# A hybrid decoder step on eight cores: weights converted by their transfers, norm weights multiplied into the normed rows, x loaded first

## The chip, the cores and the metric

The kernel runs as one program on the 8 cores of one Trainium2 chip. Each core takes one of the 8 prompt sequences and 16 of the 128 decode sequences, and no data goes between cores. The metric is device time in microseconds (us) of the slowest core. TensorE (PE) multiplies, VectorE (DVE) and ScalarE (ACT) do the elementwise work, GpSimd (POOL) builds masks and issues the transfers of its queue, SyncE (SP) issues most transfers.

## What is computed

One layer: an RMS norm, one joint input projection, two head groups in parallel (a gated linear recurrence, HGRN2, and sliding-window attention with a sink), an output projection with residual, a second norm, an MLP with squared ReLU, a last norm.

```python
def _rmsnorm(x, g):
    y = x * rsqrt(mean(x * x, -1) + EPS)
    return y * g

xn = _rmsnorm(h, ln_mix)
zq, zf, zi, zg, sq, sk, sv = split(xn @ w_in)
o_hg = rmsnorm_per_head(gla(zq, zf, zi), hg_norm) * silu(zg)
h = h + concat([o_hg, swa(sq, sk, sv, sinks)]) @ w_out
u = _rmsnorm(h, ln_mlp) @ w_up
h = h + square(relu(u)) @ w_down
y = _rmsnorm(h, ln_final)
```

x is f32, 4096 rows of 1024 per core for the prompt and 128 rows for the decode tokens. All weights come as f32; products are made in bf16.

## The kernel before

The 32 tiles of 128 prompt rows form 8 groups of 4 tiles (512 rows). The weights are 24 chunks, `wall`, of 128 x 4096 elements: 2 MB in f32, 1 MB in bf16. Chunks 0 to 5 are the input projection, 6 and 7 the output projection, 8 to 15 the up and 16 to 23 the down projection. Every group needs every chunk again, so each chunk is converted once: its bf16 form is written to `wbf` in DRAM and read back from there into a ring of 5 SBUF slots `s_wr` (`w_load`, `w_prefetch`, `w_use`, `w_release`).

The conversion goes in quarters of a chunk. `q_issue` loads 512 KB of f32 into one of four staging buffers (in `M`) on SP's queue. `q_cast` makes bf16 of it, quarters 0 and 2 on ScalarE (lines 396, 404), 1 and 3 on VectorE (lines 399, 406), and multiplies the norm weight of each row in on the way (`ln_mix`, `hg_norm`, `ln_mlp`), so that the norms themselves only scale by the inverse root. The result goes into the slot, or, for chunks that are converted ahead of use (`qc["conv"]`), into the x buffers `s_xt` and from there to `wbf`. `store` writes a slot's bf16 to `wbf`. `tick()`, called after each step of the schedule, advances this by one quarter or one store. Engines run their instructions in program order, so a cast whose quarter has not landed holds all behind it on its engine.

Order of work (`main_schedule`): (a) norms of group 0, then the input projections of groups 0 and 1 together (`head_steps`), with the norms of group 1 (`second_norms`) among them; the gate arithmetic (`gate`) runs on DVE and ACT beside the later projections. (b) Attention of group 0 alone (`back`): nothing for TensorE to do beside it. (c) For each group g: the MLP of g (`mlp_steps`) is interleaved with the attention of g+1 and the input projection of g+2 (`second`); the norms of g+2 read x tiles from `s_xt` (`xt_load`), and the residual tiles of g+2 come by `load_x`. The decode tokens ride along in group 3. Line 617 and 619 make the inverse root, line 615 the sum of squares, line 626 the scaled rows, line 633 turns them, line 635 evicts them. Line 644 and 651 are the projections and the up projection, 1247 the down projection, 1081 the output projection.

Of the kernel before, what the change touches and what calls it, by code (L numbers as in the profile page):

```python
# [6 lines left out]
F32 = mybir.dt.float32  # L7
# [159 lines left out]
def build_program(worder=None, weights=None):  # L167
# [3 lines left out]
    nc = bass.Bass("TRN2", target_bir_lowering=False, dynamic_dma_scratch_size=2048)  # L171
# [13 lines left out]
    lnmix_d = din("lnmix", [128, 8])  # L185
    lnmlp_d = din("lnmlp", [128, 8])
# [99 lines left out]
    MBYTES = 37 * 1024 + 256  # L286
    M = nc.alloc_sbuf_tensor("M", [128, MBYTES // 2], BF16)
    stg_cv = Carver(M[:, :], MBYTES)
    stg32 = [stg_cv.take([2, 512], F32) for i in range(4)]
# [46 lines left out]
    pool1(lambda e: e.affine_select(out=C.seqmask[:, :], in_=C.seqmask[:, :], pattern=[[8, 16]], base=7,
                                    channel_multiplier=-1, compare_op=ALU.is_ge, fill=0.0), [C.seqmask])
    pool1(lambda e: e.memset(C.wos[:, :], 1.0), [C.wos])
    for c in range(4):
        P.op("dve", lambda e, c=c: e.tensor_copy(out=C.wos[:, c:c + 1], in_=C.hgn[:, 0:1]), reads=[C.hgn], writes=[C.wos])  # L340
    P.op("dve", lambda e: e.tensor_tensor(out=C.dl[:, :], in0=C.lbl[:, 0:4], in1=C.lbl[:, 4:8], op=ALU.subtract),
         reads=[C.lbl], writes=[C.dl])
    P.op("act", lambda e: e.activation(out=C.lb[:, :], in_=C.dl[:, :], func=AF.Sigmoid), reads=[C.dl], writes=[C.lb])
    P.op("dve", lambda e: e.tensor_scalar(out=C.oml[:, :], in0=C.lb[:, :], scalar1=-1.0, scalar2=1.0, op0=ALU.mult,
                                          op1=ALU.add), reads=[C.lb], writes=[C.oml])
    P.op("dve", lambda e: e.tensor_scalar(out=C.noml[:, :], in0=C.lb[:, :], scalar1=-1.0, scalar2=None, op0=ALU.add),
         reads=[C.lb], writes=[C.noml])
    P.op("act", lambda e: e.activation(out=C.esinkT[:, :], in_=C.sinkT[:, :], func=AF.Exp), reads=[C.sinkT],
         writes=[C.esinkT])
    P.op("act", lambda e: e.activation(out=C.esinkB[:, :], in_=C.esinkB[:, :], func=AF.Exp), writes=[C.esinkB])  # L350
    P.op("dve", lambda e: e.tensor_scalar(out=C.homl[:, :], in0=C.oml[:, :], scalar1=0.5, scalar2=None, op0=ALU.mult),
# [29 lines left out]
    def q_cast():  # L381
# [27 lines left out]
        elif qi == 3:  # L409
            stores.append([cid, s_, 2])  # L410
# [1074 lines left out]
```

How the kernel before makes its waits and increments, by code:

```python
    def _wait(self, e, tok):  # L65
        if tok is None:
            return
        sn, v = tok
        if e is self.E["pe"] and sn == "e_pe":
            return
        if e.waited.get(sn, 0) >= v:
            return
        e.h.wait_ge(self.sems[sn], v)
        e.waited[sn] = v
# [23 lines left out]
    def op(self, en, fns, reads=(), writes=()):  # L98
        e = self.E[en]
        if callable(fns):
            fns = [fns]
        self._deps(e, reads, writes)
        ins = None
        for f in fns:
            ins = f(e.h)
        ins.then_inc(self.sems[e.semname], 1)
        e.n += 1
        tok = (e.semname, e.n)
        self._mark(tok, reads, writes)
        return tok
# [1 line left out]
    def dma(self, out, in_, reads=(), writes=(), sem=None, q="sp"):  # L112
        e = self.E[q]
        sem = sem + "_" + q
        self.dsem(sem)
        self._deps(e, reads, writes)
        ins = e.h.dma_start(out=out, in_=in_)
        ins.then_inc(self.sems[sem], 16)
        self.dcnt[sem] += 16
        tok = (sem, self.dcnt[sem])
        self._mark(tok, reads, writes)
        return tok
```

## Time and profile before

| | us |
|---|---|
| median of 3 runs | 1708.95 |
| lowest, highest | 1702.04, 1713.07 |
| the profiled execution | 1703.14 |
| its span on the slowest core (7) | 1702.1 |
| spans of the other cores | 1680.2 to 1698.6 |
| PE busy | 1537.5 (90%) |
| ACT busy, DVE busy | 961.6 (56%), 739.0 (43%) |
| DMA, mean | 183 GB/s |

"Busy" is the time in which an engine runs an instruction; matmul ends are modelled. PEclk in the rows is the granted TensorE clock as a share of 2.4 GHz. In brackets stand the idle time ahead of an instruction and what ended it. The page shows the span in 40 slices; in tenths, TensorE is busy 4785589969 in the first ten (425 us) and 8 to 9 in nearly all the rest.

### The profile page before, as it was taken

What the parts mean: (1) busy time and instruction counts of PE and PEld (TensorE: products, weight loads), DVE (VectorE), ACT (ScalarE), POOL (GpSimd) and SP (SyncE); (2) the same over time, 40 slices, a digit from 0 to 9 for tenths busy, and PEclk for the clock granted to TensorE, in tenths of its full rate; (3) what the DMA queues carried; (4) which work ended last, traced back from release to release, by engine and by line L of the source; (5) the groups of instructions that cost most, each with busy time, mean ns of one, the idle gap of its engine ahead of it and who ended that gap; (6) DMA issues with size and microseconds to landing.
All of it is one profiled execution on the core that took longest, in us unless ns stands there. A gap on an engine that the chain in (4) does not pass through costs nothing.

```text
span 1702.1 us, 26771 instructions; the slowest of 8 cores (1680.2 to 1702.1 us)
## 1 busy us (share of the span) xinstructions
PE 1537.5 (90%) x8883; PEld 745.6 (44%) x8883; DVE 739.0 (43%) x1305; ACT 961.6 (56%) x1767; POOL 76.3 (4%) x140
## 2 busy tenths in 40 slices
PE   4785589968999998899899999999999999999997
PEld 2333344423444544444455554444444444444443
DVE  2256635523544164664444435444254425343222
ACT  4656556655555655455665556555665566554433
POOL 1000000000201000110000000000000000000000
PEclk9896789988999999999999999999999999999998
DMA  8786986965745537652464334944464334634541
GB/s 242 211 266 220 250 227 230 293 201 198 260 153 139 168 106 251 216 174 87 173 213 152 118 116 163 266 176 146 164 232 173 110 151 160 227 125 168 205 154 50
DMA packets 72710, 312.01 MB, mean 183 GB/s; under 512 B 12000, under 2 KB 21216, under 8 KB 48736
## 3 DMA queue, kind: packets, MB, share of 16 engines
q1 hardware_dynamic: 46672, 257.33, 46.0%
q0 software_dynamic: 17456, 48.77, 8.3%
q10 hardware_dynamic: 8448, 4.20, 0.9%
q8 instruction: 75, 1.23, 0.3%
q14 instruction: 59, 0.48, 0.1%
HBM read 264.13 MB, written 49.15 MB: 184 GB/s over the span
## 4 chain that ended last, share of the span: by engine, by line
PE 69%; ACT 10%; DMA 8%; issue 6%; DVE 5%; SPq 0%; ACTq 0%; DVEq 0%; POOL 0%; POOLq 0%
PE pb L644 31%; PE pb L1247 24%; PE pb L1081 6%; DMA M<-wall 5%; ACT s_junk L615 2%; PE pb L651 2%; ACT s_rl L1229 2%; PE pb L633 1%; DMA s_wr<-wbf 1%; DVE XR L1251 1%; DMA wbf<-s_xt 1%; DVE U L798 1%; PE pb L904 1%; PE pb L954 1%; DMA ss<-M 1%
## 5 line engine op out<-in xcount | busy, mean ns | idle before, releaser
L644 PE MATMUL pb<-s_hnT,s_wr 128*128 128x512 bf16 x2184 | 511.5, 384 | 11.4 <-ACT M L685 3.6
L1247 PE MATMUL pb<-s_wr,s_aT 128*128 128x512 bf16 x2048 | 479.0, 382 | 25.1 <-ACT s_aT L1232 15.7
L644 PEld LDWEIGHTS pb<-s_hnT,s_wr 128*128 128x128 bf16 x2184 | 209.0, 99 | 256.3 <-issue 32.4
L1247 PEld LDWEIGHTS pb<-s_wr,s_aT 128*128 128x128 bf16 x2048 | 194.9, 98 | 262.8 <-issue 52.3
L1251 DVE TENSOR_TENSOR XR<-pb,XR 128x512 f32<-128x512 f32 x256 | 175.9, 688 | 205.0 <-PE pb L1247 197.1
L644 PE MATMUL pb<-s_xnT,s_wr 128*128 128x512 bf16 x952 | 228.8, 393 | 29.2 <-DMA s_wr<-wbf 10.1
L1229 ACT ACTIVATE s_rl<-pb 128x512 bf16<-128x512 f32 (+1 forms) x288 | 159.8, 555 | 164.6 <-PE pb L644 157.8
L1232 ACT ACTIVATE s_aT<-s_rl 128x512 bf16<-128x512 bf16 x256 | 161.2, 630 | 23.5
L644 PEld LDWEIGHTS pb<-s_xnT,s_wr 128*128 128x128 bf16 x952 | 94.0, 100 | 143.7 <-issue 46.1
L1081 PE MATMUL pb<-s_wr,s_omT 128*128 128x512 bf16 x512 | 130.0, 400 | 7.6 <-ACT s_omT L931 7.5
L615 ACT ACTIVATE s_junk<-XR 128x1024 bf16<-128x1024 f32 x72 | 75.8, 1053 | 74.3 <-DVE XR L1251 67.4
L626 DVE TENSOR_SCALAR s_xnb<-XR,s_rs 128x1024 bf16<-128x1024 f32 x40 | 30.2, 755 | 145.9 <-ACT s_rs L619 145.9
L961 ACT ACTIVATE U<-pb 128x512 bf16<-128x512 f32 x126 | 67.7, 588 | 37.6 <-PE pb L954 34.7
L1081 PEld LDWEIGHTS pb<-s_wr,s_omT 128*128 128x128 bf16 x512 | 51.2, 102 | 71.8 <-issue 19.7
L1269 DVE SCALAR_TENSOR_TENSOR XR<-XR,s_rs,s_gfin 128x1024 f32<-128x1024 f32 x32 | 41.1, 1285 | 82.4 <-ACT s_rs L619 80.0
L1084 DVE TENSOR_TENSOR XR<-pb,XR 128x512 f32<-128x512 f32 x64 | 44.1, 688 | 74.0 <-PE pb L1081 73.7
L633 PE MATMUL pb<-s_ident,s_xnb 128*128 128x128 bf16 x528 | 43.3, 229 | 35.0 <-DVE s_xnb L626 32.1
L651 PE MATMUL pb<-s_wr,s_xnT 128*128 128x512 bf16 (+2 forms) x448 | 65.9, 303 | 7.1 <-ACT U L742 4.2
L633 PEld LDWEIGHTS pb<-s_ident,s_xnb 128*128 128x128 bf16 x528 | 36.4, 102 | 50.4 <-issue 39.1
L840 ACT ACTIVATE U<-pb,s_epsc 128x512 f32<-128x512 f32 x33 | 22.5, 682 | 56.2 <-PE pb L838 49.8
L117 POOL DMA_DIRECT2D y<-XR x32 | 17.4, 543 | 818.7 <-DVE XR L1269 301.4
L685 ACT ACTIVATE U<-pb 128x512 bf16<-128x512 f32 x56 | 33.2, 596 | 36.4 <-PE pb L644 35.5
(209 smaller groups left out, 1457.5 us busy)
## 6 DMA issues: line engine op xcount, KB each, us to landing
s_wr<-wbf SPq DMA_DIRECT2D x167, 1024.0 KB, 5.9
M<-wall SPq DMA_DIRECT2D x96, 512.0 KB, 8.7
wbf<-s_wr SPq DMA_DIRECT2D x19, 1024.0 KB, 8.8
y<-XR POOLq DMA_DIRECT2D x32, 512.0 KB, 3.6
s_xt<-x POOLq DMA_DIRECT2D x24, 512.0 KB, 6.0
XR<-x POOLq DMA_DIRECT2D x24, 512.0 KB, 7.5
wbf<-s_xt SPq DMA_DIRECT2D x20, 256.0 KB, 7.2
XR<-x SPq DMA_DIRECT2D x8, 512.0 KB, 12.6
```

The lines of the kernel that those rows point to most:

```text
L615: P.op("act", lambda e: e.activation(out=junk[:, :], in_=src[:, :], func=AF.Square, accum_out=ssq[:, 0:1]), reads=[src], writes=[ssq, junk])
L633: P.op("pe", [lambda e, k=k: e.transpose(bkb[:, k * 128:(k + 1) * 128], xb[:, k * 128:(k + 1) * 128], C.ident[:, :]) for k in range(8)], r ...
L644: P.op("pe", [lambda e, k=k: e.matmul(bk[0:ncols, 0:TB], lhsT=W[:, k, col0:col0 + ncols], rhs=srcT[:, k, 0:TB], start=(k == 0), stop=(k == ...
L651: P.op("pe", [lambda e, k=k: e.matmul(bk[:, 0:ncols], lhsT=srcT[:, k, j * 128:(j + 1) * 128], rhs=W[:, k, c0:c0 + ncols], start=(k == 0), ...
L961: P.op("act", lambda e, pt=pt, bk=bk: e.activation(out=pt[:, :], in_=bk[:, :], func=AF.Exp, scale=0.125), reads=[bk], writes=[pt])
L1081: P.op("pe", [lambda e, k=k: e.matmul(bk[:, :], lhsT=B.omT[:, k, j * 128:(j + 1) * 128], rhs=W[:, k, :], start=(k == 0), stop=(k == 7)) fo ...
L1084: P.op("dve", lambda e: e.tensor_tensor(out=xs_[:, nh * 512:(nh + 1) * 512], in0=bk[:, :], in1=xs_[:, nh * 512:(nh + 1) * 512], op=ALU.add ...
L1229: P.op("act", lambda e, bk=bk, rl=rl, TB=TB: e.activation(out=rl[:, 0:TB], in_=bk[:, 0:TB], func=AF.Relu), reads=[bk], writes=[rl])
L1232: P.op("act", lambda e, fl=fl, rl=rl, TB=TB, B=B: e.activation(out=B.aT[:, fl, 0:TB], in_=rl[:, 0:TB], func=AF.Square), reads=[rl], writes ...
L1247: P.op("pe", [lambda e, f=f, B=B, j=j, W=W, bk=bk: e.matmul(bk[:, :], lhsT=B.aT[:, f, j * 128:(j + 1) * 128], rhs=W[:, f, :], start=(f == ...
L1251: P.op("dve", lambda e, nh=nh, bk=bk, xs_=xs_: e.tensor_tensor(out=xs_[:, nh * 512:(nh + 1) * 512], in0=bk[:, :], in1=xs_[:, nh * 512:(nh ...
L1269: P.op("dve", lambda e: e.scalar_tensor_tensor(out=xs_[:, :], in0=xs_[:, :], scalar=rs[:, 0:1], in1=C.gfin[:, :], op0=ALU.mult, op1=ALU.mu ...
```

## The change

1. Conversion. Staging buffers, `q_issue`, `q_cast` and all casts on ScalarE and VectorE go. `w_load` of a chunk that is not converted yet is one transfer on POOL's queue, f32 in DRAM to the bf16 slot; the store to `wbf` stays. 11 chunks go this way. The other 13 are converted by `convert()`: one transfer on POOL's queue from `wall` to `wbf`, DRAM to DRAM, one at every third step of stage (b); POOL waits ahead of it for all of TensorE's work so far and for the last transfer but one.
2. Norm weights. `norm_pre` multiplies the full f32 row `gmix` or `gmlp` (128 x 1024, loaded on ACT's queue) in with a scalar_tensor_tensor instead of the tensor_scalar; `hg_norm` is multiplied in where `t1` is made, by another scalar_tensor_tensor. The sum of squares writes its unused output into `s_xnb` instead of `s_junk`.
3. Start. Four x tiles are the first issues of SP; the small constants follow. POOL issues the first two chunks ahead of its constants, the next three behind them. The ops on the gate constants come behind group 0's norms.
4. x tiles of groups 2 and (residuals) 2 go on SP's queue instead of POOL's. The decode tokens' x comes through `s_xt` and once more into `M` for the residual.
5. Smaller masks for the decode tokens, broadcast in the instruction. The descriptor scratch of POOL's queue is doubled, `M` is 7 KB smaller.

```diff
-    nc = bass.Bass("TRN2", target_bir_lowering=False, dynamic_dma_scratch_size=2048)
+    nc = bass.Bass("TRN2", target_bir_lowering=False, dynamic_dma_scratch_size=4096)
...
         if cid in converted:
...
+            P.dma(dst, wbf_d[cid], reads=[wbfb[cid]], writes=[wring[s_]], sem="wr%d" % s_)
         else:
             converted.add(cid)
-            qload.extend((cid, s_, qi) for qi in range(4))
-            while qload and len(qcast) < 4:
-                q_issue()
+            P.dma(dst, wall_d[cid], writes=[wring[s_]], sem="wc%d" % s_, q="pool")
+            stores.append([cid, s_, 2])
+
+    def convert():
+        for cid in WORDER[wr["next"]:]:
+            if cid not in converted:
+                converted.add(cid)
+                e = P.E["pool"]
+                P._wait(e, ("e_pe", P.E["pe"].n))
+                if len(straight) > 1:
+                    P._wait(e, straight[-2])
+                straight.append(P.dma(wbf_d[cid], wall_d[cid], writes=[wbfb[cid]], sem="cd%d" % (len(straight) % 2),
+                                      q="pool"))
+                return
...
-    def norm_pre(src):
-        rs = norm_stats(src)
+    def norm_pre(src, gain):
...
         xb = xnb[xnb_free.pop(0)]
-        P.op("dve", lambda e: e.tensor_scalar(out=xb[:, :], in0=src[:, :], scalar1=rs[:, 0:1], scalar2=None,
-                                              op0=ALU.mult), reads=[src, rs], writes=[xb])
+        rs = norm_stats(src, xb)
+        P.op("dve", lambda e: e.scalar_tensor_tensor(out=xb[:, :], in0=src[:, :], scalar=rs[:, 0:1], in1=gain[:, :],
+                                                     op0=ALU.mult, op1=ALU.mult), reads=[src, rs, gain], writes=[xb])
...
         xs[0] = [load_x(n) for n in gtiles(0)]
+        P.dma(C.gmix.ap, gmix_d, writes=[C.gmix], sem="gmix", q="act")
+        w_prefetch(2)
+        const_ops()
         w_prefetch()
+        const_loads()
         xs[1] = [load_x(n) for n in gtiles(1)]
...
-        tk["every"] = 2
         qc["conv"] = True
```

The rows of the program show the places. First SP at the start of the program, in the form of a difference (- before, + after; `XR` holds the residual tiles of x):

```order
-L117 DMA s_lnmix<-lnmix 128x8
-L117 DMA s_lnmlp<-lnmlp 128x8
+L117 DMA XR<-x 128x1024 x4
 L117 DMA s_lbl<-lbl 128x8
 L117 DMA s_hgn<-hgn 128x1
@@ -6,77 +5,20 @@
 L117 DMA s_esinkB<-sinkB 128x8
 L117 DMA XR<-x 128x1024 x4
-L117 DMA M<-wall 128x1024 x4
-L117 DMA XR<-x 128x1024 x4
-L117 DMA M<-wall 128x1024 x6
```

The first four x tiles moved from behind six small transfers to the front, and the f32 quarters (`M<-wall`) left SP. Next POOL in the changed kernel, from its last start constant to its first transfers in stage (c):

```order
L331 MEMSET s_S_bf 128x512
L117 DMA s_wr<-wall 128x4096 x9
L117 DMA wbf<-wall 32x16384 x13
L117 DMA s_xt<-x 128x1024 x2
L117 DMA s_gfin<-gfin 128x1024
```

Where POOL had no transfer before stage (c), it now has 22; each direct one is written as 32 rows of 16384 elements, 64 KB of f32 each. Last ScalarE in stage (b), attention of the first tiles, before:

```order
L404 CAST s_xt<-M 128x1024
L833 ACTIVATE U<-pb 128x512
L881 CAST s_S_bf<-Sst 128x512
L404 CAST s_xt<-M 128x1024
L829 COPY U<-pb 128x512
L615 ACTIVATE s_junk,s_ssq<-XR 128x1024
L617 ACTIVATE s_tv<-s_ssq,s_epsc 128x1
```

and the same place in the changed kernel:

```order
L771 ACTIVATE U<-pb 128x512
L819 CAST s_S_bf<-Sst 128x512
L767 COPY U<-pb 128x512
L545 ACTIVATE s_xnb,s_ssq<-XR 128x1024
L547 ACTIVATE s_tv<-s_ssq,s_epsc 128x1
```

The two weight casts (`s_xt<-M`) are gone; the rest stands in the same order. TensorE's rows are the same in both kernels throughout, up to line numbers.

## Rows read from the trace of the kernel before

**Rows 1.** Table by stretches of the slowest core: busy us of each engine, instructions.

```profile
core 7: us, PE busy (x) PEld busy (x) DVE busy (x) ACT busy (x) POOL busy (x), PEclk, DMA share, GB/s
...
150.00:225.00 75.00, 43.33 (x265) 22.95 (x263) 42.78 (x92) 39.85 (x71) 0.00 (x0) 0.68 0.88 249
...
340.00:400.00 60.00, 41.24 (x177) 17.76 (x176) 13.86 (x24) 32.38 (x48) 0.98 (x2) 0.77 0.65 215
...
450.00:1702.00 1252.00, 1193.63 (x7060) 583.01 (x7059) 544.12 (x940) 699.85 (x1314) 58.80 (x99) 0.99 0.48 164
```

**Rows 2.** Timeline, first 60 us: start, length, engine, line, instruction, [idle before <-releaser].

```profile
1.05 0.39 SPq L117 DMA_DIRECT2D s_lnmix<-lnmix  x1
...
3.86 1.94 SPq L117 DMA_DIRECT2D XR<-x  x4
...
16.17 1.04 ACT L615 ACTIVATE s_junk<-XR 128x1024 bf16<-128x1024 f32 x1
...
20.18 0.69 DVE L635 COPY s_xnT<-pb 128x1024 bf16<-128x1024 bf16 x1 [0.67 <-PE pb L633]
...
24.22 9.88 PE L644 MATMUL pb<-s_xnT,s_wr 128*128 128x512 bf16 x32 [4.15 <-DVE s_wr L399]
...
37.41 4.97 PE L644 MATMUL pb<-s_xnT,s_wr 128*128 128x512 bf16 x16 [3.31 <-DVE s_wr L399]
...
58.28 1.01 PE L633 MATMUL pb<-s_ident,s_xnb 128*128 128x128 bf16 x8 [4.30 <-DVE s_xnb L626]
```

**Rows 3.** Timeline, 104 to 225 us: end of the gate arithmetic, a cast on ScalarE.

```profile
105.64 3.27 PE L644 MATMUL pb<-s_hnT,s_wr 128*128 128x512 bf16 x8 [3.55 <-ACT M L685]
...
148.10 0.88 DVE L399 TENSOR_SCALAR s_wr<-M,s_lnmlp 128x512 bf16<-128x512 f32 x2 [2.23 <-ACT s_wr L396]
...
149.33 0.58 PE L819 MATMUL pb<-U 128*128 128x128 bf16 x4 [1.87 <-DVE s_vS_all L775]
...
159.13 1.04 ACT L404 CAST s_wr<-M 128x1024 bf16<-128x1024 f32 x1 [5.50 <-DMA M<-wall]
```

**Rows 4.** Groups by line, 150 to 225 us: weight casts of ScalarE and VectorE.

```profile
L396 ACT ACTIVATE s_xt<-M,s_lnmlp 128x512 bf16<-128x512 f32 x8 | 5.3, 714 | 5.3 <-DMA wbf<-s_xt 5.3
L404 ACT CAST s_xt<-M 128x1024 bf16<-128x1024 f32 x5 | 5.2, 1045 | 5.6 <-DMA wbf<-s_xt 5.6
...
L399 DVE TENSOR_SCALAR s_xt<-M,s_lnmlp 128x512 bf16<-128x512 f32 x8 | 3.5, 480 | 0.0
```

**Rows 5.** Timeline, 350 to 400 us: a cast on ScalarE and the three stops of TensorE.

```profile
355.77 1.04 ACT L404 CAST s_wr<-M 128x1024 bf16<-128x1024 f32 x1 [7.77 <-DMA M<-wall]
...
358.60 6.50 PE L644 MATMUL pb<-s_xnT,s_wr 128*128 128x512 bf16 x16 [8.45 <-ACT s_aT L1232]
...
380.57 3.57 PE L644 MATMUL pb<-s_xnT,s_wr 128*128 128x512 bf16 x8 [5.12 <-DMA s_wr<-wbf]
389.33 3.57 PE L1247 MATMUL pb<-s_wr,s_aT 128*128 128x512 bf16 x8 [5.19 <-DVE s_wr L406]
```

**Rows 6.** Page, DMA queues, q1: packets, MB, share of 16 engines.

```profile
q1 hardware_dynamic: 46672, 257.33, 46.0%
```

**Rows 7.** DMA view, 542 to 544 us: the cache loads that convert f32 to bf16.

```profile
q0 software_dynamic: 997, 0.29, 129.4%
```

**Rows 8.** DMA view, 1078 to 1082 us: two queues at once.

```profile
q1 hardware_dynamic: 108, 0.78, 71.9%
q0 software_dynamic: 93, 0.38, 23.6%
```

**Rows 9.** DMA view, 1084 to 1092 us: DRAM to DRAM copies in q1.

```profile
q1 hardware_dynamic: 39, 1.29, 72.3%
```

**Rows 10.** Timeline, 248 us: first norm of the third group of tiles.

```profile
248.40 1.06 ACT L615 ACTIVATE s_junk<-s_xt 128x1024 bf16<-128x1024 f32 x1 [0.70 <-DMA s_xt<-x]
```

**Rows 11.** Page, costliest groups: norm scaling and final norm on VectorE.

```profile
L626 DVE TENSOR_SCALAR s_xnb<-XR,s_rs 128x1024 bf16<-128x1024 f32 x40 | 30.2, 755 | 145.9 <-ACT s_rs L619 145.9
...
L1269 DVE SCALAR_TENSOR_TENSOR XR<-XR,s_rs,s_gfin 128x1024 f32<-128x1024 f32 x32 | 41.1, 1285 | 82.4 <-ACT s_rs L619 80.0
```

More of the change, by code:

```diff
@@ L285, in build_program @@
     rl_p = [sb("rl%d" % i, [512], BF16) for i in range(2)]
-    MBYTES = 37 * 1024 + 256
+    MBYTES = 30 * 1024 + 256
     M = nc.alloc_sbuf_tensor("M", [128, MBYTES // 2], BF16)
-    stg_cv = Carver(M[:, :], MBYTES)
-    stg32 = [stg_cv.take([2, 512], F32) for i in range(4)]
     UBYTES = 37 * 1024
@@ L336, in build_program @@
[L336 to L349, printed above, removed]
@@ L381, in q_cast @@
-    def q_cast():
-        cid, s_, qi, st = qcast.pop(0)
-        sc = C.lnmix if cid < 6 else (C.wos if cid < 8 else (C.lnmlp if cid < 16 else None))
-        en = ("act", "dve")[qi % 2]
-        if s_ is None:
-            dst = cq[qc["c"] % 4]
-            while any(t_[1] is None and t_[4] is dst for t_ in stores):
-                store(stores.pop(0))
-            qc["c"] += 1
-            dap = dst.ap
-        else:
-            dst = wring[s_]
-            dap = dst[:, 2 * qi:2 * qi + 2, :]
-        if sc is not None:
-            if en == "act":
-                fns = [lambda e, k=k: e.activation(out=dap[:, k, :], in_=st[:, k, :], func=AF.Identity,
-                                                   scale=sc[:, 2 * qi + k:2 * qi + k + 1]) for k in range(2)]
-            else:
-                fns = [lambda e, k=k: e.tensor_scalar(out=dap[:, k, :], in0=st[:, k, :],
-                                                      scalar1=sc[:, 2 * qi + k:2 * qi + k + 1], scalar2=None,
-                                                      op0=ALU.mult) for k in range(2)]
-            P.op(en, fns, reads=[st, sc], writes=[dst])
-        elif en == "act":
-            P.op(en, lambda e: e.copy(out=dap, in_=st[:, :, :]), reads=[st], writes=[dst])
-        else:
-            P.op(en, lambda e: e.tensor_copy(out=dap, in_=st[:, :, :]), reads=[st], writes=[dst])
-        if s_ is None:
-            stores.append([cid, None, 2, qi, dst, (qc["c"] - 1) % 4])
-        elif qi == 3:
-            stores.append([cid, s_, 2])
@@ L434, in w_load @@
         cid = WORDER[l]
-        while any(q[0] == cid for q in qload + qcast):
-            q_step()
         if any(wslot_free[0] == t_[1] or t_[0] == cid for t_ in stores):
@@ L473, in tick @@
         w_prefetch()
-        if qc["conv"] and not qload and not record:
-            for cid in WORDER[wr["next"]:]:
-                if cid not in converted:
-                    converted.add(cid)
-                    qload.extend((cid, None, qi) for qi in range(4))
-                    break
-            while qload and len(qcast) < 4:
-                q_issue()
+        if qc["conv"] and not record and tk["i"] % tk["every"] == 0:
+            convert()
     def w_use(cid):
@@ L493, in w_use @@
             wr["next"] += 1
-        while any(q[0] == cid for q in qload + qcast):
-            q_step()
         w_prefetch()
@@ L524, in carve @@
         K.rd8 = two.take([8], F32)
+        K.kt_smp = two.take([512], BF16)
         share(one, two)
```

264 lines of the change are left out of this document (124 added, 140 removed).

## The prediction

> **What bounds the kernel now.** I read four views. The table by stretches comes first: from 450 us to the end TensorE is busy 1193.6 of 1252 us at a granted clock of 0.99 of full speed [rows 1]. The TensorE rows stand in the same order in both kernels, so nothing is to be had there, about three quarters of the time. In 150 to 225 us, attention of group 0 alone, TensorE is busy 43.3 of 75 us at 0.68, VectorE 42.8 and ScalarE 39.9: no engine is full, so a chain of operations from engine to engine sets the pace. In 340 to 400 us TensorE is busy only 41.2 of 60 us, at 0.77. The time to be had lies in the first 400 us.
>
> The timeline says what the chain waits for there. The first projection, at 24.22, waited for a weight cast on VectorE though the last normed rows were evicted at 20.87; the second chunk's, at 37.41, waited 3.31 us for one too; at 58.28 a transpose waited 4.30 us for normed rows that stood behind casts [rows 2]. At 105.64 TensorE waited 3.55 us for an eviction that ScalarE had behind a cast whose f32 quarter was late [rows 3]. In stage (b) ScalarE stood still 5.5 us at 159.13 for a quarter [rows 3], and 5.3 and 5.6 us for staging space whose store to `wbf` was not through [rows 4]. From 350 to 390 the same thing comes three times: a cast waits 7.77 us for its quarter, the eviction behind it is late, TensorE stops for 8.45, 5.12 and 5.19 us [rows 5]. The waits come from casts that stand in the program order of two engines ahead of work that others need.
>
> **The change part by part.** I count against the profiled execution (1703.14; the median is 1708.95, so 5.8 is added at the end).
>
> *Start.* The first x tiles were issued at 3.86 behind six small transfers, the first of them at 1.05 [rows 2]; now they lead, 2.8 us earlier. But `wall` and `gmix` now come beside them from another queue. The main queue moves 257.33 MB in 46.0% of 16 engines' 1702 us, 20.5 GB/s an engine, 330 on 16 [rows 6]. If the queues share by bytes, 2.1 MB of x, as much of `wall` and 0.5 of `gmix` land at 3 + 4.7/0.33 = 17.3. From the last Square to the end of the last eviction it was 16.17 to 20.87, 4.7 us [rows 2]; the scaling becomes a scalar_tensor_tensor, whose nearest row takes 1285 ns against 755 [rows 11], so 5.2. First projection at 22.6 instead of 24.22: **-1.6**. The second chunk is then there: **-3.3**. Casts among the second norms: three stops of 3 to 4.3 us [the longest in rows 2], of which the slower scaling and the later x tiles leave most; I take **-3.0** and not 10.
>
> *Gates, 105 to 149.* The 3.55 us at 105.64 go. Between 105 and 150 stand 12 casts of 0.48 on VectorE and 13 of 0.71 on ScalarE (durations of rows 4), 5.8 and 9.2 us, in a chain that uses both engines by turns; half of them, 7.3, is on it. The end waits for `s_vS_all` behind two halves at 148.10 [rows 3], 3.5 us. Sum **-14.4**.
>
> *Attention of group 0.* The 5.5 us at 159.13 go whole. Of the 10.9 us behind staging stores [rows 4] I take 6, since some fall where ScalarE had nothing due. Cast time is 5.3 + 5.2 on ScalarE, 3.5 on VectorE for the half shown and about as much for the plain casts, with those into slots some 22 us; a quarter on the chain, 5.5. Sum **-17**. The bounds are 5.5 (only the first wait counts) and 5.5 + 10.9 + 22 = 38 (everything was on it).
>
> *Stage (c).* The stops sum to 18.8 us; behind them 32 matmuls went in 6.50 + 3.57 + 3.57 = 13.6 us, 0.43 each [rows 5], which is the low clock (the mean granted clock of the stretch is 0.77 [rows 1]); at the full one they take half, so 6.8 more. 25.6 together; I take **-24**. By then all weights are converted, if the direct transfers are done.
>
> *What it adds.* 66 scalings (two for each of 32 tiles and for the decode tokens) cost 0.53 us each more [rows 11]; VectorE has the room beside the MLP (544 of 1252 us busy [rows 1]). Where a head waits for a norm, in the first tiles, some count: **+3**; if no cover were left it would be 35. `t1` by scalar_tensor_tensor and `hg_norm`: the same element count as before, nothing; its cover is TensorE waiting elsewhere. Contention of the new traffic with loads that TensorE needs: **+2**, a choice between nothing and the first rival. x tiles 1 and 2 of group 2 now stand on SP behind two slot loads that wait for TensorE's release; SP has nothing else due, and the tiles were needed at 248.40 [rows 10], so nothing. Masks and constants are off the path.
>
> *The direct transfers.* This is the price that no row has. 13 chunks go from f32 to bf16 DRAM to DRAM in rows of 64 KB, two per engine and chunk, one every third step from about 147 us; the first x tile of group 2 would be wanted at 248.4 less what was gained, 22, so at 226. The nearest row for the rate: cache loads that convert write 0.29 MB in 2 us with the queue full [rows 7], 0.58 MB of f32 read, 290 GB/s, 7.2 us for 2 MB. 13 x 7.2 = 94 us of engine time from 147 on: end at 241 if nothing else ran. The other traffic of stage (b) is small, and x tiles don't wait for the conversions if queues share by bytes. From rows the two queues share packet by packet: 93 packets of 4.1 KB in one beside 108 of 7.2 KB in the other, 4 us, both with work [rows 8]. The Trainium skill, DMA: Bandwidth & Descriptors, "Queues, rings and completion order", says the same, that an engine takes turns between queues a packet at a time; by that rule, were a 64 KB row one packet, the forecast turns into the first rival. What the forecast rests on is that the software queue cuts its rows: the mean packet there is 4.1 KB though rows are 4 KB, which fits both. I give cutting into small pieces a bit over half.
>
> Sum: -1.6 -3.3 -3.0 -14.4 -17 -24 +3 +2 = -58.3, so 1644.8 for a profiled execution and **1650** for the median. Own range: -47 with attention at -5.5; -76 with attention at -27 (all waits, half the cast time) and the second norms at -10. On the median's scale 1633 to 1662.
>
> **The rivals.** *Big packets.* If rows of 16 KB and 64 KB are one packet each, every 4 KB packet of x waits for 16 KB of weights: 0.8 + 0.2 us at 20.5 GB/s, 32 times per engine, x lands at 3 + 32 = 35 and the first projection starts at 40. All five chunks are there, so no more stops: the gates end some 5 us earlier than before, not 22. The direct rows: copies of 61 KB in the main queue give 39 packets, 1.29 MB, 72.3% of 8 us, 2.4 us each and, with 18 big and 21 small of 0.43, 4.6 us for a big one [rows 9]. A round of one 64 KB row and one 8 KB packet takes 3.6 us (3.2 + 0.4 at 20.5 GB/s) up to 5.0 (4.6 + 0.4). 26 rounds end at 147 + 26r: 241 to 277. The x tiles of group 2 sit behind two slot loads in the main queue, 16 + 16 rounds, so land about 3 us behind the end of all conversions. First norm at 244 to 280 instead of 226, and the sum is -22 (start to attention) -24 +3 +(18 to 54) = -25 to +11: 1684 to 1720, middle 1700. For it: rows 9 has such packets as wholes. Against: those are of the hardware queue.
>
> *Slower.* The same mechanism with a dearer round, since f32 to bf16 in DRAM writes back what it reads. It decides at 269 us, r = 4.7: there the gain is used up. Over r = 5.4 (end at 287) it is more than 1% slower, 1726; at 6.2 the end is 308 and the time 1748. Loads of `s_wr` that cross it come over 20 us after issue, since all of their eight packets an engine then wait for a 64 KB row each. No row excludes a round of 6.2.
>
> *Half.* Both waits shrink but the chain of gates and attention is its own bound: attention -5.5, gates -7, stops -17, the rest as above: 1674.
>
> *The change does nothing for the stops.* `s_wr` loads come late by the direct transfers instead of by casts. Then -58.3 + 24 = -34, again near 1674; I put it with *Half*.
>
> **How the numbers follow.** Forecast 0.52, big packets 0.24, slower 0.13, half 0.11. A measurement of this kernel can tell 1% from no change, 17 us: below 1692 is faster, above 1726 slower. Faster: 0.52 + 0.11 and of big packets only where r is below 3.9, 0.03: 0.66. Same: 0.21. Slower 0.13. The range goes from 1634 over the half case into big packets up to 1706, which leaves out the slower rival and the upper third of big packets.
>
> **What would show it.** Right: the first L644 matmul (new number of the line) near 22 us and no stop at the second chunk; packets of the software queue of 4 KB while `wall` loads; no cast of `M` on ScalarE or VectorE; stage (b) of 55 to 60 us at a clock above 0.68; no TensorE stop above 3 us between 330 and 400; the first norm of group 2 near 226. Wrong: packets of 16 or 64 KB in the software queue and the first projection at 40 us; `s_xt<-x` on SP landing over 20 us after issue, and TensorE idle ahead of group 2's transposes; `wbf<-wall` still running at 250. The prediction falls with the step on how rows are cut.

## The result

The changed kernel takes 1724.01 us against 1708.10 before, medians of seven runs each. In some executions, whichever the kernel, the cores of one die run at a lower clock and the time is longer; all ratios, and all times from here on, leave these out, and since the profiled execution of the changed kernel is one of them (cores 4 to 7), its rows are read on core 0 (span 1717.9). The ratio is 1.0079, with a 95% interval of 1.0053 to 1.0105: 0.8% slower, 13.5 us (about 1720 against 1708). The forecast was 1650, with a range to 1706. The time lies outside it, on the other side of before. The first rival, big packets (1684 to 1720), comes nearest, right where it meets the second (slower, from 1726 on).

Where times of before and after are set beside each other below, both are core 0's, unless core 7 is named. The page first (it is that of the slowest core, 4; core 0 has the same packets): the two queues, q1 the main one of SP and q0 that of POOL (packets, MB, share of the engines), then issues with KB each and median us to landing.

```profile
q1 hardware_dynamic: 30832, 205.94, 34.1%
q0 software_dynamic: 18656, 70.26, 18.3%
...
wbf<-wall POOLq DMA_DIRECT2D x13, 1024.0 KB, 20.9
s_wr<-wall POOLq DMA_DIRECT2D x11, 1024.0 KB, 13.0
wbf<-s_wr SPq DMA_DIRECT2D x11, 1024.0 KB, 22.2
```

The main queue moves 51 MB less than in [rows 6], and a conversion takes 13 to 21 us to land. The table by stretches of core 0:

```profile
core 0: us, PE busy (x) PEld busy (x) DVE busy (x) ACT busy (x) POOL busy (x), PEclk, DMA share, GB/s
...
150.00:225.00 75.00, 57.84 (x349) 28.84 (x347) 34.64 (x67) 33.90 (x65) 2.95 (x6) 0.81 1.01 128
225.00:340.00 115.00, 52.35 (x266) 23.29 (x263) 24.97 (x46) 23.86 (x46) 2.46 (x5) 0.72 0.77 144
340.00:400.00 60.00, 57.15 (x355) 28.44 (x354) 24.83 (x43) 34.59 (x62) 1.61 (x3) 1.00 0.39 139
...
450.00:1702.00 1252.00, 1206.49 (x7146) 588.52 (x7144) 569.11 (x946) 708.62 (x1328) 56.12 (x99) 0.99 0.50 168
```

Two stretches have improved as forecast. In 150 to 225 TensorE is busy 57.8 us at 0.81 (before 43.8 at 0.72; core 7 in [rows 1] 43.3 at 0.68), and in 340 to 400 57.2 us at 1.00 (before 38.5 at 0.80; core 7 41.2 at 0.77): attention is faster and the three stops of [rows 5] are gone. But in 225 to 340 TensorE is busy 52.4 of 115 us, where core 0 before had 111.0. What stands there:

```profile
291.45 1.06 ACT L545 ACTIVATE s_xnb<-s_xt 128x1024 bf16<-128x1024 f32 x1 [66.19 <-DMA s_xt<-x]
...
232.58 3.57 PE L1187 MATMUL pb<-s_wr,s_aT 128*128 128x512 bf16 x8 [5.68 <-DMA s_wr<-wbf]
...
295.41 1.18 PE L893 MATMUL pb<-M,s_kT_all 64*128 64x512 bf16 x2 [56.60 <-DVE XR L1191]
```

ScalarE waited 66.2 us for the first x tile of group 2, and TensorE stood still 56.6 us behind it. Before, core 0 began this norm at 242.96. A loss at the start is seen in the timeline too: the four first norms, an activation on the constants, the first norm of group 1, then the first projection and the transposes behind that norm.

```profile
7.92 1.06 ACT L545 ACTIVATE s_xnb<-XR 128x1024 bf16<-128x1024 f32 x1
...
14.82 1.06 ACT L545 ACTIVATE s_xnb<-XR 128x1024 bf16<-128x1024 f32 x1 [5.02 <-DMA XR<-x]
...
23.23 1.06 ACT L545 ACTIVATE s_xnb<-XR 128x1024 bf16<-128x1024 f32 x1 [6.57 <-DMA XR<-x]
...
31.18 1.06 ACT L545 ACTIVATE s_xnb<-XR 128x1024 bf16<-128x1024 f32 x1 [6.12 <-DMA XR<-x]
...
47.13 0.20 ACT L334 ACTIVATE s_esinkT<-s_sinkT 128x4 f32<-128x4 f32 x1 [14.13 <-DMA s_esinkB<-sinkB]
...
52.71 1.05 ACT L545 ACTIVATE s_xnb<-XR 128x1024 bf16<-128x1024 f32 x1
...
36.49 13.46 PE L574 MATMUL pb<-s_xnT,s_wr 128*128 128x512 bf16 x48 [0.94 <-DVE s_xnT L565]
...
57.34 1.01 PE L563 MATMUL pb<-s_ident,s_xnb 128*128 128x128 bf16 x8 [7.39 <-DVE s_xnb L556]
```

The four x tiles come 7 to 8 us apart and the first projection starts at 36.49 instead of 25.07 (core 0 before; 24.22 on core 7, [rows 2]). Then ScalarE stands 14.1 us for the small constants, which were issued by 5.6 us. The norms of group 1 stand behind them in its program, and TensorE stops for these, 7.4 us at 57.34.

A ledger of one core shows where time is won and lost. Each line is the start of the same sum of squares in both timelines of core 0 (the how-manieth of 99, and what it reads):

| norm | before | after | difference |
|---|---|---|---|
| 4, last tile of group 0 | 17.02 | 31.18 | +14.2 |
| 8, last tile of group 1 | 53.49 | 64.24 | +10.7 |
| 12, last one of attention of group 0 | 214.78 | 195.82 | -19.0 |
| 13, first x tile of group 2 | 242.96 | 291.45 | +48.5 |
| 17 | 308.47 | 357.95 | +49.5 |
| 23 | 429.58 | 453.73 | +24.2 |
| 95 | 1570.28 | 1598.12 | +27.8 |

So: 14 lost at the start, 30 won between 53 and 215 us, 67 lost at one x tile, 25 won at the stops. Everything that the casts cost was given back, as forecast; two waits for x took more.

The end of this ledger, +27.8, is twice the 13.5 us of the whole. The metric is the slowest core, and core 0 before was not it (1690.1 us, core 7 1702.1), while core 0 after is the longest of its die. The ledger tells where time goes; the size of the whole is the ratio's to tell.

### The profile page after: what moved, and what is told of

The parts are those of the page before. It is cut to its first block, busy times and chain, and to the rows that moved or that the text cites. A ratio compares the mean times of both kernels' runs of the same rounds, so it can differ in the third digit from the quotient of the medians.

```text
span 1783.1 us, 26077 instructions; the slowest of 8 cores (1705.9 to 1783.1 us)
## 1 busy us (share of the span) xinstructions
PE 1582.6 (89%) x8713; PEld 762.1 (43%) x8883; DVE 737.0 (41%) x1221; ACT 910.2 (51%) x1687; POOL 78.9 (4%) x153
## 4 chain that ended last, share of the span: by engine, by line
PE 73%; ACT 8%; DMA 5%; DVE 5%; issue 4%; another core or an unknown queue 4%; ACTq 0%; SPq 0%; DVEq 0%; POOL 0%; POOLq 0%
PE pb L574 34%; PE pb L1187 24%; PE pb L1021 7%; DMA s_esinkB<-sinkB 2%; PE pb L581 2%; DMA s_wr<-wbf 1%; ACT s_xnb L545 1%; PE pb L563 1%; ACT s_rl L1169 1%; DVE U L730 1%; PE pb L893 1%; PE pb L842 1%; DMA ss<-M 1%; ACT s_aT L1172 1%
## 5 line engine op out<-in xcount | busy, mean ns | idle before, releaser
L574 PE MATMUL pb<-s_hnT,s_wr 128*128 128x512 bf16 x2126 | 527.2, 398 | 12.9 <-ACT U L771 2.5
L1187 PE MATMUL pb<-s_wr,s_aT 128*128 128x512 bf16 x1986 | 501.8, 401 | 26.8 <-ACT s_aT L1172 11.5
L574 PEld LDWEIGHTS pb<-s_hnT,s_wr 128*128 128x128 bf16 x2184 | 215.0, 101 | 268.4 <-issue 108.4
L1187 PEld LDWEIGHTS pb<-s_wr,s_aT 128*128 128x128 bf16 x2048 | 202.3, 102 | 281.4 <-issue 140.8
L1172 ACT ACTIVATE s_aT<-s_rl 128x512 bf16<-128x512 bf16 x256 | 161.2, 630 | 24.7 <-ACT s_rl L1169 1.5
L545 ACT ACTIVATE s_xnb<-XR 128x1024 bf16<-128x1024 f32 x72 | 75.9, 1054 | 94.2 <-DVE XR L1191 69.1
L556 DVE SCALAR_TENSOR_TENSOR s_xnb<-XR,s_rs,s_gmlp 128x1024 bf16<-128x1024 f32 x32 | 41.1, 1283 | 122.4 <-ACT s_rs L549 122.4
L900 ACT ACTIVATE U<-pb 128x512 bf16<-128x512 f32 x126 | 67.9, 589 | 40.9 <-PE pb L893 39.1
L556 DVE SCALAR_TENSOR_TENSOR s_xnb<-s_xt,s_rs,s_gmix 128x1024 bf16<-128x1024 f32 x25 | 32.1, 1284 | 131.7 <-ACT s_rs L549 131.7
L563 PEld LDWEIGHTS pb<-s_ident,s_xnb 128*128 128x128 bf16 x528 | 37.9, 105 | 72.6 <-issue 63.6
L581 PE MATMUL pb<-s_wr,s_xnT 128*128 128x128 bf16 (+2 forms) x447 | 66.1, 306 | 0.1
L545 ACT ACTIVATE s_xnb<-s_xt 128x1024 bf16<-128x1024 f32 x25 | 26.2, 1047 | 66.0 <-DMA s_xt<-x 66.0
```

The costliest lines, as they stand in the source:

```text
L545: P.op("act", lambda e: e.activation(out=scrap[:, :], in_=src[:, :], func=AF.Square, accum_out=ssq[:, 0:1]), reads=[src], writes=[ssq, scrap])
L556: P.op("dve", lambda e: e.scalar_tensor_tensor(out=xb[:, :], in0=src[:, :], scalar=rs[:, 0:1], in1=gain[:, :], op0=ALU.mult, op1=ALU.mult) ...
L563: P.op("pe", [lambda e, k=k: e.transpose(bkb[:, k * 128:(k + 1) * 128], xb[:, k * 128:(k + 1) * 128], C.ident[:, :]) for k in range(8)], r ...
L574: P.op("pe", [lambda e, k=k: e.matmul(bk[0:ncols, 0:TB], lhsT=W[:, k, col0:col0 + ncols], rhs=srcT[:, k, 0:TB], start=(k == 0), stop=(k == ...
L581: P.op("pe", [lambda e, k=k: e.matmul(bk[:, 0:ncols], lhsT=srcT[:, k, j * 128:(j + 1) * 128], rhs=W[:, k, c0:c0 + ncols], start=(k == 0), ...
L900: P.op("act", lambda e, pt=pt, bk=bk: e.activation(out=pt[:, :], in_=bk[:, :], func=AF.Exp, scale=0.125), reads=[bk], writes=[pt])
```

## The experiments

Times are medians, and ratios are to the kernel before in the same session (medians of 1703 to 1706 us) with 95% intervals (that of both_small is wide because it rests on two runs). A ratio need not be the quotient of the two medians to the last digit. All rows are of core 0. The edits are written out; the kernels make the pieces of a transfer in a helper.

| kernel | us | ratio |
|---|---|---|
| direct_halves | 1669.0 | 0.9773 (0.9720 to 0.9827) |
| slot_quarters | 1707.5 | 1.0006 (0.9973 to 1.0040) |
| both_small | 1653.0 | 0.9677 (0.9588 to 0.9766) |
| x_early | 1712.6 | 1.0050 (1.0008 to 1.0092) |
| direct_32k | 1706.1 | 0.9997 (0.9976 to 1.0018) |
| x_ahead_of_slots | 1717.5 | 1.0080 (1.0054 to 1.0105) |
| small_no_direct | 1636.9 | 0.9611 (0.9573 to 0.9648) |
| small_no_weights | 1653.1 | 0.9670 (0.9647 to 0.9694) |
| small_x_early | 1650.7 | 0.9665 (0.9648 to 0.9681) |
| small_x_every2 | 1652.7 | 0.9704 (0.9666 to 0.9742) |
| small_scratch2k | 1654.5 | 0.9717 (0.9670 to 0.9763) |
| before_x_first | 1711.4 | 1.0025 (0.9993 to 1.0056) |

### direct_halves: the direct rows shorter

```diff
-straight.append(P.dma(wbf_d[cid], wall_d[cid], ...))
+for i in range(2):
+    c = slice(2048 * i, 2048 * (i + 1))
+    e.h.dma_start(out=wbf_d[cid][:, c], in_=wall_d[cid][:, c]).then_inc(sem, 16)
```

> The changed kernel, but each of the 13 direct transfers is two, of 128 rows of 8 KB f32 (4 KB bf16) instead of 32 rows of 64 KB. Theory P (long packets): an x tile of eight rows per engine stands in the main queue behind one 64 KB row (4.7 us) for each of its rows and of those of two slot loads ahead of it; with 8 KB rows a turn is about 0.8 us, the first norm of group 2 (x at 291 us in the changed kernel, 243 before, core 0) comes at 225 to 240, and the whole at 1655 to 1675. Start as in the changed kernel (first projection at 36 us). Theory B (bytes): the 13 chunks' f32 bytes fill the engines whatever their rows are (97% of stage (b)); the norm stays at 280 or later and the time within 8 us of 1722.

1669.0. The first norm of group 2 starts 67 us earlier than in the changed kernel (1 us earlier than the range expected) and waits for nothing:

```profile
223.98 1.05 ACT L545 ACTIVATE s_xnb<-s_xt 128x1024 bf16<-128x1024 f32 x1
```

Theory P holds, B falls: the same bytes are converted, and the last conversion even lands later, at 336 us instead of 291. How the engines were shared is seen in the DMA view from 200 to 240 us, when both queues have work. First the changed kernel:

```profile
q0 software_dynamic: 182, 3.87, 83.5%
q1 hardware_dynamic: 179, 1.34, 14.7%
```

Then direct_halves:

```profile
q0 software_dynamic: 759, 2.77, 54.0%
q1 hardware_dynamic: 762, 4.54, 45.3%
```

In both, the two queues have sent the same number of packets, 182 and 179, 759 and 762: they take turns one packet at a time, whatever its size. In the changed kernel a turn gives 7.5 KB of the main queue for 21 KB of bf16 written by a conversion (packets of 4 bytes counted in: 3.87 MB are 118 rows of 32 KB written, the other 64 are small), and the main queue moves 1.34 MB in 40 us; with 8 KB rows it moves 4.54.

### direct_32k: between the two

```diff
+o2, i2 = (d_.rearrange("(a h b) m -> h a (b m)", h=2, b=2) for d_ in (wbf_d[cid], wall_d[cid]))
+for i in range(2): dma_start(out=o2[i], in_=i2[i])
```

> The changed kernel, but each direct transfer is two of 32 rows of 32 KB f32, between the 64 KB of the change and the 8 KB of direct_halves. By the packet theory one of our 4 to 8 KB packets waits for one such row per turn: about 2.4 us (half of the 4.7 us of a 64 KB row) plus 0.4. The first x tile of group 2 has 24 packets per engine to go in the main queue (two slot loads of eight, x of eight) from about 195 us: 24 x 2.8 = 67, so its norm comes near 262 us (291 with 64 KB, 224 with 8 KB), and the time lies between, 1690 to 1702. If there is a threshold and not a turn for each row (rows over some size block, others share), it is like one of the two: 220 to 230 and 1668, or 285 and more and 1720.

1706.1 and a first norm at 249.5; below it the DMA view from 200 to 240 us:

```profile
249.46 1.06 ACT L545 ACTIVATE s_xnb<-s_xt 128x1024 bf16<-128x1024 f32 x1 [26.03 <-DMA s_xt<-x]
```

```profile
q0 software_dynamic: 331, 3.60, 75.7%
q1 hardware_dynamic: 335, 2.20, 23.8%
```

331 packets beside 335, and 2.20 MB of the main queue: between the two, so there is no threshold. The expected 262 was 12 too late and the expected total 4 too low. The second norm came at 294.56, 45 us behind the first instead of 25 as before, though its tile had landed at 265.5: it stands in the program behind work that waited for TensorE, and TensorE had stopped 15.7 us for a slot load that landed at 283.7, which I had not counted.

### x_ahead_of_slots and x_early: the place in the queue

x_ahead_of_slots issues the two x tiles just ahead of the two slot loads instead of behind:

```diff
+if k == 38:
+    P._wait(P.E["sp"], ("e_pe", P.E["pe"].n))
+    xq.extend([xt_load(xahead.pop(0)), xt_load(xahead.pop(0))])
```

> The changed kernel, direct rows of 64 KB kept, but the two x tiles of group 2 stand ahead of the two slot loads in the main queue, issued at about the same time (190 us). It counts turns apart from size: the first tile now has 8 packets per engine to go instead of 24, the second 16 instead of 32. At 5.1 us a turn: the first norm at 190 + 41 + 3 = 234 (291 in the changed kernel), the second near 275 (318). The slot loads then come only with the end of the direct transfers, so TensorE stops for them near 290 and the whole stays within 10 us of the changed kernel, 1708 to 1722. If a queue with long packets takes the engines for as long as it has work (no turns), the first norm stays at 285 or later.

```profile
192.18 1.05 SPq L117 DMA_DIRECT2D s_xt<-x  x2
193.40 4.58 SPq L117 DMA_DIRECT2D s_wr<-wbf  x2
...
230.04 1.06 ACT L545 ACTIVATE s_xnb<-s_xt 128x1024 bf16<-128x1024 f32 x1 [5.81 <-DMA s_xt<-x]
...
288.17 3.57 PE L1187 MATMUL pb<-s_wr,s_aT 128*128 128x512 bf16 x8 [62.30 <-DMA s_wr<-wbf]
```

Issued at 192.2, the first tile is there at 230.0: 8 packets per engine took 38 us, 4.7 each. What stands in the queue first, second and third lands after 38, 68 and 96 us (x tile, x tile, slot load); in the changed kernel it was 39, 72 and 98 us (slot load, slot load, x tile). An x tile is half the bytes of a slot load, in as many rows: it is the number of turns that counts. TensorE then stopped 62.3 us for the slot load that had lost its place, and the time is the changed kernel's, 1717.5. x_early issues them some 50 us ahead, before the attention:

```diff
+xq.extend([xt_load(xahead.pop(0)), xt_load(xahead.pop(0))])
 qc["conv"] = True
```

> The changed kernel, but the first two x tiles of group 2 are issued ahead of the attention of group 0 and so ahead of all direct transfers. Theory P: only what crosses the long packets is late; the first two norms of group 2 come at 215 to 230 instead of 291, but the two slot loads (landing 54 to 81 us after issue in the changed kernel) and the later x tiles still cross them, so TensorE stops for these instead: 1690 to 1712. If x alone was the trouble: 1655 to 1675. Theory B as stated for the other runs says the same as P here.

1712.6, just above the range of P. The first norm came at 221.8 as expected, the second only at 303.57: its tile was there at 164, but in the program it stands behind work of TensorE that had stopped. The stops are now all for slot loads, 48 us together:

```profile
228.22 3.57 PE L1187 MATMUL pb<-s_wr,s_aT 128*128 128x512 bf16 x8 [4.71 <-DMA s_wr<-wbf]
...
261.89 3.57 PE L574 MATMUL pb<-s_hnT,s_wr 128*128 128x512 bf16 x8 [23.10 <-DMA s_wr<-wbf]
...
293.29 3.57 PE L574 MATMUL pb<-s_hnT,s_wr 128*128 128x512 bf16 x8 [20.60 <-DMA s_wr<-wbf]
```

### slot_quarters and both_small: the start

```diff
-P.dma(dst, wall_d[cid], writes=[wring[s_]], ..., q="pool")
+for i in range(4):
+    c = slice(1024 * i, 1024 * (i + 1))
+    e.h.dma_start(out=dst[:, c], in_=wall_d[cid][:, c]).then_inc(sem, 16)
```

> The changed kernel, but each of the 11 loads of wall into a slot is four, of 128 rows of 4 KB f32 (2 KB bf16) instead of 16 KB rows. Theory P: the four x tiles land by 17 to 20 us instead of 31, the first projection starts at 24 instead of 36.5, and since the direct transfers start 12 us earlier too, all that follows is 10 to 12 us earlier: 1708 to 1714. Theory B: the bytes ahead of x are the same, the projection stays at 33 or later, 1720. Third (descriptors): four times as many packets of a quarter cost more in all, the chunks come late, a stop of 3 us or more at the second or third chunk, 1720 to 1735.

1707.5, half a us below the range of P. The first projection is at 23.55, after a wait of 0.94 us for the last evicted rows and none for a chunk:

```profile
23.55 12.99 PE L574 MATMUL pb<-s_xnT,s_wr 128*128 128x512 bf16 x47 [0.94 <-DVE s_xnT L565]
```

The changed kernel, 0 to 20 us, shows why:

```profile
q0 software_dynamic: 220, 1.67, 56.6%
q1 hardware_dynamic: 400, 1.51, 27.3%
```

The software queue's 1.67 MB written are 204 packets of 8 KB, 56.6% of 320 us of engine time, 0.89 us each; those of x take 0.22, so a round is 1.1 us at most. The main queue is ahead here because the software queue sent nothing until 6 us. From 8 to 20 us the counts are equal:

```profile
q0 software_dynamic: 194, 1.46, 80.2%
q1 hardware_dynamic: 194, 0.73, 19.5%
```

194 rounds of 16 engines in 12 us are 0.99 us each; a tile has 8 rows an engine, and 8 us are the distance of the tiles. Then come the four small constants, 128 rows of 4 to 32 bytes each. The same view from 31 to 40 us:

```profile
q0 software_dynamic: 208, 1.47, 97.4%
q1 hardware_dynamic: 207, 0.00, 2.8%
```

They take as many turns as four x tiles. They landed from 37.9 to 47.1, and the x tiles of group 1 behind them from 49.2 on.

> Both cuts at once: slot loads in rows of 4 KB f32, direct ones in rows of 8 KB. Theory P: the two gains add, 1640 to 1662, which is what was forecast for the change; first projection at 24, first norm of group 2 at 215 to 230, no stop of TensorE over 3 us between 330 and 400. Theory B: not below 1710. If the gain of one eats that of the other (less than 10 us beside the better of the two alone), the start isn't on the path to the end.

```profile
23.37 12.61 PE L574 MATMUL pb<-s_xnT,s_wr 128*128 128x512 bf16 x47 [0.94 <-DVE s_xnT L565]
...
206.90 1.05 ACT L545 ACTIVATE s_xnb<-s_xt 128x1024 bf16<-128x1024 f32 x1
...
246.15 3.52 PE L1187 MATMUL pb<-s_wr,s_aT 128*128 128x512 bf16 x8 [11.72 <-DMA s_wr<-wbf]
```

1653.0, inside the range; the first norm of group 2, at 206.9, is 8 us earlier than expected. The starts of the same norms as in the ledger, both_small against before: +1.0, -5.8, -37.2, -36.1, -21.4, -46.1, and -47.2 for the 95th. The gains add, and 11.7 us of TensorE are lost to one slot load at 246. The stops from 340 on are gone, and the stretch from 150 to 225 us is fuller than in the changed kernel because attention begins and ends 17 to 18 us earlier:

```profile
core 0: us, PE busy (x) PEld busy (x) DVE busy (x) ACT busy (x) POOL busy (x), PEclk, DMA share, GB/s
...
150.00:225.00 75.00, 61.22 (x349) 29.34 (x355) 33.00 (x61) 35.27 (x68) 7.18 (x14) 0.88 1.00 156
225.00:340.00 115.00, 95.84 (x551) 46.26 (x560) 43.49 (x74) 53.79 (x98) 5.70 (x11) 0.96 0.90 195
340.00:400.00 60.00, 59.38 (x313) 28.26 (x318) 27.93 (x39) 42.00 (x73) 3.72 (x11) 1.00 0.64 217
```

### small_no_direct: what the conversion traffic still costs

Made from both_small; the 13 direct transfers are not issued, and the loads of those chunks read the stored chunk 2.

> The kernel with small rows, without the 13 direct transfers: their chunks are read from the stored copy of another chunk, so this part of the weights is left out. It shows what the direct traffic still costs once rows are short. The second and third x tile and the slot loads of group 1 and 2 were late in both_small (the lead over before fell from 37 us at 178 to 21 us at 287 and came back to 46 by 345). Theory, the traffic costs 8 to 15 us yet: 1638 to 1646. Rival, none of it is on the path, since what is late is caught up in slack (as the forecast's +2 says): 1650 to 1655.

1636.9, 16 us below both_small and 1 us below the range of the theory. The two were run in different sessions; on core 0 the 17th norm starts 14.6 us earlier than in both_small. The lead over before does not fall after 215 (norm 14 at -35.3, 17 at -36.1, 23 at -62.5), so the traffic's cost is on the path: the theory holds and the forecast's +2 does not. That reading one stored chunk again and again is no faster by itself was not tested.

### small_no_weights: what the norms cost

Made from both_small, without the multiplications with the norm weights (`t1` likewise, not shown).

```diff
-scalar_tensor_tensor(out=xb, in0=src, scalar=rs, in1=gain, op0=ALU.mult, op1=ALU.mult)
+tensor_scalar(out=xb, in0=src, scalar1=rs, scalar2=None, op0=ALU.mult)
```

> The kernel with small rows in both kinds of transfer, but the norm weights are left out altogether: the scaling of the normed rows is the tensor_scalar of the kernel before (0.76 us) instead of the scalar_tensor_tensor (1.28 us), and t1 the tensor_tensor. It shows what the multiplication in the norms costs. As in the prediction's sum (+3): 2 to 6 us faster than both_small (1653), most of it in the first 225 us. Rival, that a head waits for every norm (0.53 us x 66): 20 us or more faster. Rival, that VectorE hides it all: within 1 us.

1653.1 against 1653.0, in two sessions; the intervals alone would not exclude a few us. The ledger of core 0 is finer: norms 8 and 12 start within 0.2 us of those of both_small, the first of group 2 is 1.8 us earlier, and the 17th is 1.6 us later. The forecast's +3 is not there.

### small_x_early, small_x_every2, small_scratch2k

> Small rows in both kinds, and the first two x tiles of group 2 issued ahead of the attention of group 0. In both_small the first norm of group 2 came at 207 us and the second at 232 (core 0), both after waits for x; in the changed kernel with x early the first came at 222 us where the attention had ended, some 22 us earlier than before. Here the tiles lie in SBUF by 150: 2 to 12 us faster than both_small, if TensorE doesn't stop instead for the slot load that it now meets 11.7 us too early (L1187 <- s_wr<-wbf in both_small); in that case within 2 us of it.

1650.7: 2 us below both_small, which the intervals don't tell apart. The expectation had misread both_small: its first norm of group 2 waited for nothing (the row above has no wait, the tile had landed at 205.0), and here it starts at 207.5. The 15th norm is 12 us earlier, and TensorE loses that again at slot loads. It is the lowest median of all kernels that leave nothing out.

> small_x_early with a direct transfer at every second step instead of every third. The transfers wait for each other anyway (two outstanding; landing 24 us each, DMA share 0.99 from 150 to 300), so if the engines' throughput sets their end the rhythm does nothing: within 2 us of 1650. If gaps in the issue had left the engines idle: up to 6 us faster.

1652.7, 2 us above small_x_early, in another session: no gain is seen from the rhythm of the issues, as expected if the engines' throughput sets the end.

> both_small with the descriptor scratch of the software queue at 2048 as in the kernel before, instead of 4096. If the larger scratch matters: GpSimd's issues wait for room in the ring (one issue of 7 us and more instead of 0.55), slot loads late at the start, 3 to 15 us slower. If not: within 2 us of both_small (1653).

1654.5, not to be told from both_small. GpSimd does wait ahead of the last six of the start's quarters, which it doesn't in both_small (the profile names no releaser; room for descriptors is the likely one), but the chunks concerned are not due:

```profile
20.99 2.13 POOL L118 DMA_DIRECT2D s_wr<-wall  x4 [4.29 <-issue]
31.54 1.06 POOL L118 DMA_DIRECT2D s_wr<-wall  x2 [8.41 <-issue]
```

### before_x_first: the order at the start alone

```diff
+for n in range(4):
+    P.dma(xres[n].ap, x_d[n * 128:(n + 1) * 128, :], writes=[xres[n]], sem="x%d" % n)
 for b, d_ in cl:
     P.dma(b.ap, d_, writes=[b], sem="cst")
...
+        if n < 4:
+            return b_
```

> The kernel before with one edit: the four first x tiles are issued ahead of the six small constants. In the prediction's sum the start is bound by the first chunk's casts (the first projection waited 4.15 us for one), so -2.8 us for x is at most -1 to 0 at the first projection, and the whole within 2 us of before. If x were the bound: the first projection at 21.4 and the whole 3 us faster. If the first norm only waits for the constants' activations on ScalarE, its time (10.2 us) does not move.

```profile
15.51 1.28 ACT L345 ACT_TABLE_LOAD   x1 [15.51 <-DVE s_dl L343]
...
18.54 1.04 ACT L617 ACTIVATE s_junk<-XR 128x1024 bf16<-128x1024 f32 x1
...
31.80 8.59 PE L646 MATMUL pb<-s_xnT,s_wr 128*128 128x512 bf16 x32 [4.15 <-DVE s_wr L401]
```

The first norm moved from 10.2 to 18.5 and the first projection from 25.07 to 31.80: later, not earlier. The constants now land behind 2 MB of x, and ScalarE has the activations on them ahead of the first norm in its program. Of that only a part reaches the end (1.0025, which includes no change), as some of the later waits shrink: on core 0 the three stops of TensorE between 354 and 385 us sum to 14.4 us instead of 21.1. It was none of the outcomes that I had written down. The change moves those activations behind the norms of group 0, but not out of the way: they wait until 47.13 in the changed kernel, with the norms of group 1 behind them, and with small slot rows until 25.1.

## Why the prediction was wrong

**What bounds the kernel.** Right. The casts in program order ahead of needed work were the cost, and with short rows (both_small) the change brings 50 us by the medians of that session, 55 by the ratio. One reading was loose: of the three stops in [rows 5] the middle one, 5.12 us, waited for a slot load from `wbf` and not for a cast. It is gone too; the runs don't show why.

**Start: -1.6, -3.3, -3.0.** Wrong for the change: +14.2 at the fourth norm. The term has x in at 17.3 "if the queues share by bytes"; they share by packets, and the fourth tile landed at 31.0. "Masks and constants are off the path" is wrong too: the constants' rows take turns like any others, ScalarE waited 14.1 us for them, and TensorE 7.4 us behind it. With small slot rows it is right within a few us: first projection 1.7 us earlier, -5.8 in sum at norm 8 against -7.9.

**Gates -14.4 and attention -17.** 31.4 together; measured between norms 8 and 12: 29.7 in the changed kernel, 31.4 in both_small. I don't read the exact match as more than luck: the forecast was made from core 7, where this stretch was 4 us longer before than on core 0, and half of the casts' 15.0 us is 7.5, not 7.3. But the size was right.

**Stops -24.** 25.3 in the changed kernel (norms 17 to 23), 24.7 in both_small.

**Norm scaling +3.** Nothing found (small_no_weights).

**The direct transfers.** This is the step that failed. The prediction rested on "that the software queue cuts its rows", and gave it "a bit over half", though its only row for it, a mean packet of 4.1 KB in [rows 8] from rows that were 4 KB anyway, "fits both". Nothing spoke for one side, and the x tiles of group 2 were put at "nothing" on it; they cost 67 us. Rows of 64 KB went as one packet, 32 KB written, each; [rows 9] had shown such packets in the main queue, and I had set them aside as another queue's. (The 39 packets there are 21 of 61,440 bytes, 4.4 us each, and 18 of 4 bytes, and not 18 and 21; that lowers the rival's 4.6 a little.) GpSimd's issues in the changed kernel give the round:

```profile
250.28 0.49 POOL L117 DMA_DIRECT2D wbf<-wall  x1 [9.81 <-DMA wbf<-wall]
261.54 0.49 POOL L117 DMA_DIRECT2D wbf<-wall  x1 [10.77 <-DMA wbf<-wall]
```

11.3 us from issue to issue, 10.5 on the mean from 239.98 to 271.47, are two rounds of 5.2 us (the rival had 3.6 to 5.0, and its turning point at 4.7). The last direct transfer landed at 291; the rival's sum with 291 for the norm is -43 + 65 = +22, the measured +13.5 (+27.8 on core 0). The rival had the mechanism, both places and nearly the size. Its chance, 0.24, and that of *Slower*, 0.13, were too small, and the range left them out.

**Contention +2.** Wrong even with short rows: 16 us between both_small and small_no_direct, and on core 0 direct_halves too loses 16 us of its lead between norms 14 and 17 (-19.0 to -3.1). Conversions and loads share the same 16 engines, whose share is 1.00 and 0.90 in the two stretches from 150 to 340 us in both_small, and slot loads that TensorE needs at 246 come 11.7 us late. That 1653 comes so near to 1650 is luck in part: the steps of both_small on core 0 sum to -47 and not -58, and the forecast added them to a kernel before of 1708.95, which was at 1703 in that session.

The Trainium skill, DMA: Bandwidth & Descriptors, "Queues, rings and completion order", says that an engine switches queues only after a whole packet; the equal counts above agree. It puts 9 to 17 descriptors into a typical packet. Here a turn was one row: had the 8 rows per engine of a tile gone in one turn, it would have landed behind one or two conversion rows; it took 8 turns of 4.7 us (x_ahead_of_slots), and rows of 4 to 32 bytes took a turn each as well. For these two queues the measurement decides against that number.

**What stays open.** Why the middle stop of [rows 5] is gone, how much the start would gain if the constants came after the x tiles of group 1 or in fewer rows, and how much of both_small's remaining 16 us another order of the slot loads could recover; small_x_early only moved the stops (2.3 to 3.4 us each, three of them).

## What to carry to other kernels

The two queues of this kernel shared the DMA engines by packet, not by byte, and a packet was a whole contiguous row, whether of 4 bytes or of 64 KB. Before a bulk copy is put beside loads that an engine waits for, write it with rows of the size of the loads' own, and count a small constant's rows, not its bytes; here cutting the rows of the two kinds of transfers turned 0.8% slower into 3.2% faster, with no other edit. When a forecast hangs on one unknown, ask of each row whether it could have looked otherwise if the answer were the other one.

## What the runs showed of the hardware

- A DRAM to DRAM conversion of 64 KB f32 rows took one turn of 4.5 us per row (3.87 MB are 118 rows, 83.5% of 640 us of engine time), 5.2 with the other queue's turn, with equal packet counts in the two queues (182 and 179 in 40 us). 32 KB rows: 331 and 335. 8 KB rows: 759 and 762. In these 40 us 3.87, 3.60 and 2.77 MB were written by the conversions and 1.34, 2.20 and 4.54 MB moved by the main queue.
- A transfer of 128 tiny rows takes as many turns as one of 128 long rows: in the changed kernel the four constants of 0.5 to 4 KB, issued within 5.6 us, landed from 37.9 to 47.1 us, behind x tiles that were there at 31.0 (207 packets with 0.00 MB beside 208 of the other queue from 31 to 40 us). In before_x_first, with no second queue beside them, they were there at 14.4, behind 2 MB of x.
- A contiguous chunk of 128 x 4096 is issued as 32 rows of 16384 elements when source and destination are both whole in DRAM. The shape that the code writes is not the shape that goes out; the program's rows show it.
